# Attention of a hybrid decoder layer: copies, turns and scores in an interleaved order, and the 16-key meta tile's weighted sums as split fp32r products

## The reference

```python
score = jnp.einsum('bqhs,bqh->bqs', jax.nn.relu(logits), w_idx)      # indexer
_, sel = lax.top_k(score, topk)                                      # topk = 128 keys
s = jnp.einsum('bqhc,bqkc->bqhk', q_lat, kv_sel) * (ATT_HEAD_DIM ** -0.5)
p = jax.nn.softmax(jnp.where(valid, s, -jnp.inf), axis=-1)
o_lat = jnp.einsum('bqhk,bqkc->bqhc', p, kv_sel)
y_att = jnp.einsum('bthc,hcd->bthd', o_lat, w_uv)
```

## Time and profile before

| | us |
|---|---|
| median of 3 runs (range) | 1017.39 (1017.03 to 1017.8) |
| the profiled execution's own time | 1017.49 |
| its span in the trace | 1015.8 |
| PE busy | 996.9, 98% of the span |
| DVE, ACT, POOL busy | 714.0, 493.8, 118.1 |
| first score of the attention, first output product behind it | 529.5, 600.1 |

### The profile page before, as it was taken

The page is one execution under the profiler, slowest core; times in us unless marked ns, Lnnn a source line. Parts: engine busy times, 40 slices in busy tenths (PEclk is TensorE's granted clock), DMA queues, the critical chain, the costliest instruction groups (busy, mean ns, idle before and its releaser), DMA issues.

```text
span 1015.8 us, 18999 instructions
## 1 busy us (share of the span) xinstructions
PE 996.9 (98%) x7028; PEld 907.9 (89%) x7028; DVE 714.0 (70%) x1317; ACT 493.8 (49%) x868; POOL 118.1 (12%) x92
## 2 busy tenths in 40 slices
PE   9999999999999999999999999999999999999996
PEld 8999999999999988699765668889999999988886
DVE  6988888887322264699997523699989889942236
ACT  6656665566121264546346522576656665812121
POOL 0000000001121262045302205320000000000000
PEclk9999999999999999999999999999999999999999
DMA  7233332323223313132110102113323232333212
GB/s 252 84 100 107 102 105 90 116 80 105 86 86 111 113 44 116 36 123 82 44 42 1 43 1 83 43 42 126 124 83 124 85 121 96 125 103 101 98 57 84
DMA packets 30849, 90.48 MB, mean 89 GB/s; under 512 B 4689, under 2 KB 5329, under 8 KB 30801
## 3 DMA queue, kind: packets, MB, share of 16 engines
q1 hardware_dynamic: 30800, 89.83, 26.7%
HBM read 87.72 MB, written 2.10 MB: 88 GB/s over the span
## 4 chain that ended last, share of the span: by engine, by line
PE 81%; DVE 15%; ACT 2%; issue 1%; DMA 0%; SPq 0%; DVEq 0%; ACTq 0%
PE ps L1229 38%; PE ps L1287 22%; PE ps L1152 9%; DVE sc L2201 3%; DVE top L2200 3%; PE ps L1714 2%; PE ps L1424 1%; PE ps L1692 1%; DVE qk L2240 1%; PE ps L1705 1%; DVE wlo L1877 1%; PE ps L1489 1%; PE ps L1722 1%; PE ps L1337 1%; PE ps L1335 1%
## 5 line engine op out<-in xcount | busy, mean ns | idle before, releaser
L1229 PE MATMUL ps<-tsum,whi 128*128 128x264 f32 (+1 forms) x1280 | 243.1, 282 | 0.5 <-ACT ht L790 0.5
L1229 PEld LDWEIGHTS ps<-tsum,whi 128*128 128x128 f32 x1280 | 202.3, 188 | 0.7 <-issue 0.7
L1229 PE MATMUL ps<-tsum,wlo 128*128 128x264 f32 (+1 forms) x640 | 180.3, 282 | 0.0
L1229 PE MATMUL ps<-xh,whi 128*128 128x264 f32 (+1 forms) x480 | 135.4, 282 | 0.3 <-ACT sil L790 0.3
L1229 PE MATMUL ps<-xl,whi 128*128 128x264 f32 (+1 forms) x480 | 135.5, 282 | 0.0
L1229 PE MATMUL ps<-xh,wlo 128*128 128x264 f32 (+1 forms) x480 | 135.3, 282 | 0.0
L729 ACT ACTIVATE whi<-wraw 128x1408 fp32r<-128x1408 f32 (+1 forms) x48 | 74.6, 1555 | 123.0 <-PE ps L1287 123.0
L1787 DVE TENSOR_TENSOR wlo<-wraw,whi 128x1408 fp32r<-128x1408 f32 (+1 forms) x38 | 70.0, 1843 | 85.3 <-ACT whi L729 85.3
L1287 PE MATMUL ps<-hh,whi 128*128 128x264 f32 (+1 forms) x462 | 124.2, 323 | 0.0
L1287 PE MATMUL ps<-hh,wlo 128*128 128x264 f32 (+1 forms) x462 | 123.5, 322 | 0.0
L1287 PE MATMUL ps<-hl,whi 128*128 128x264 f32 (+1 forms) x462 | 123.4, 321 | 0.0
(11 more groups left out here) (287 smaller groups left out, 1828.0 us busy)
## 6 DMA issues: line engine op xcount, KB each, us to landing
wraw<-in_ffn_w_gate SPq DMA_DIRECT2D x43, 512.0 KB, 4.2
wraw<-in_ffn_w_up SPq DMA_DIRECT2D x42, 512.0 KB, 4.3
wraw<-in_ffn_w_down SPq DMA_DIRECT2D x32, 384.0 KB, 3.2
wraw<-in_ffn_w_down SPq DMA_DIRECT2D x32, 320.0 KB, 3.5
wraw<-in_w_in SPq DMA_DIRECT2D x19, 512.0 KB, 4.5
wraw<-in_w_out SPq DMA_DIRECT2D x8, 512.0 KB, 4.4
out<-zrow SPq DMA_DIRECT2D x8, 256.0 KB, 2.0
x<-in_x SPq DMA_DIRECT2D x3, 528.0 KB, 7.5
```

Source lines behind the costliest of these rows:

```text
L1229: mm = pe.matmul(ps[:, bank, 0:(HT, HALF_SEQ)[p // 2]], w[:, k * P:(k + 1) * P], v[:, k, :], start=(first and k == 0 and n == 0), stop=(k ...
```

## The change

**Order.** In all three `attention()` loops a round is cut finer: two scores, two turns, one score, the weigh of the meta tile, turn 2, one score, and then the other weighs and turns. ACT makes its copies of tiles 0 and 1 behind the exponentials of heads 0 and 1, that of tile 2 behind head 2, the rest behind head 3; DVE's copies move in the same way, `normalise` goes behind the third `masked`, and the mLSTM pieces and the late selection rounds go to a round's end.

**Meta tile.** Its weighted sum becomes a split product. The transposes of tile 0 take 32 key columns instead of 16 (`META_ROWS`); ACT copies the turned bank as fp32r into partitions 0 to 31 of `pt_h`, DVE subtracts that copy from the bank and puts the rest into partitions 32 to 63. PE makes one fp32r matmul with `clo` (low part of the latents) over 16 partitions, and one with `meta_c`, which holds the high part twice (partitions 0 to 15 and 32 to 47, zeros elsewhere), over 64 partitions. ACT makes `chi` once (16x128), POOL makes `clo` and `meta_c` once (`split_latents`). Tiles 1 to 4 stay plain fp32.

**Memory.** `c_parts` and `pts` lie over `cs` and `v1` with another type; two of the four score buffers move (`sbuf[2]`, `sbuf[3]`).

```diff
-HEAD_GATED = ((1, 0), (1, 1), (2, 1), (3, 1))
-HEAD_HI = ((1, 1), (2, 0), (3, 0), (4, 0))
+HEAD_GATED = (1, 1, 2, 3)
+HEAD_HI = (2, 2, 3, 4)
...
-LATE_AT = ((4, 0), (4, 1), (5, 0))
+LATE_AT = (4, 4, 5)
...
+META_ROWS = 32
...
-        sbuf = [sil[:, 0, :], sil[:, 1, :], pt_flat[:, 1024:1024 + T], pt_flat[:, 1024 + T:1024 + 2 * T]]
+        sbuf = [sil[:, 0, :], sil[:, 1, :], pt_flat[:, 2048:2048 + T], qk[:, 3, :]]
...
+                def split_latents():
+
+                    pool.wait_ge(c_hi, 1)
+                    pool.wait_ge(ct_turned, 1)
+                    m = N_META
+                    pool.tensor_tensor(clo[0:m, 0, :], cmat[0:m, 0, :], chi[0:m, 0, :].bitcast(F32), ALU.subtract).then_inc(c_lo, 1)
...
                 mix_lo(9)
+                split_latents()
                 causal_mask(3)
...
                 act.activation(ct[:, END[3]:T], ps[:, 5, 0:P], ACT.Copy).then_inc(ct_ready, 1)
+                act.activation(chi[0:N_META, 0, :], cmat[0:N_META, 0, :], ACT.Copy).then_inc(c_hi, 1)
                 hi(MIX0 + 4, 0, UW, False)
...
+                        if i and t % 2 == 0:
+                            continue
+                        act.wait_ge(pt_turned, t + 1)
+                        if t >= 2:
+                            act.wait_ge(pv_step, t - 1)
+                        dst, src = (pt[t % 2], ps[:, t % 2, :]) if i else (pt_h[t % 2][0:META_ROWS, :], ps[0:META_ROWS, t % 2, :])
+                        act.activation(dst, src, ACT.Copy).then_inc(pt_hi, 1)
...
                 def weigh(G, i):
                     t = TP0[G] + i
-                    pe.wait_ge(pt_even if t % 2 == 0 else pt_odd, t // 2 + 1)
-                    if i == 0 and G >= 1:
-                        pe.wait_ge(ol_ready, G)
-                    pe.matmul(ps[:, 3, :], cmat[0:ROWS[i], i, :], pt_flat[0:ROWS[i], (t % 2) * 512:(t % 2 + 1) * 512],
-                              start=(i == 0), stop=(i == 1 + G // 2)).then_inc(pv_step, 1)
+                    if i == 0:
+                        pe.wait_ge(pt_hi, copies_by_act(t))
+                        if G >= 1:
+                            pe.wait_ge(ol_ready, G)
+                        pe.wait_ge(c_lo, 3)
+                        m = N_META
+                        pe.matmul(ps[:, 3, :], clo[0:m, 0, :], pt_h[t % 2][0:m, :], start=True, stop=False)
+                        copied_weights(t)
+                        pe.matmul(ps[:, 3, :], meta_c[:, :], pt_h[t % 2][0:64, :], start=False, stop=False).then_inc(pv_step, 1)
+                        return
+                    copied_weights(t)
+                    pe.matmul(ps[:, 3, :], cmat[:, i, :], pt[t % 2], start=False, stop=(i == 1 + G // 2)).then_inc(pv_step, 1)
...
+                        turn(G - 1, 0)
+                        turn(G - 1, 1)
+                    if G < GROUPS:
+                        scores(4 * G + 2)
+                    if G >= 1:
+                        weigh(G - 1, 0)
+                        if last_tile >= 2:
+                            turn(G - 1, 2)
+                    if G < GROUPS:
+                        scores(4 * G + 3)
+                    if G >= 1:
+                        for i in range(1, last_tile + 1):
                             weigh(G - 1, i)
+                            if i + 2 <= last_tile:
+                                turn(G - 1, i + 2)
...
-                        if t % 2 == 0:
+                        if i == 0:
+                            dve.wait_ge(pt_hi, copies_by_act(t))
+                            ins = dve.tensor_tensor(pt_h[t % 2][32:32 + META_ROWS, :], ps[0:META_ROWS, t % 2, :],
+                                                    pt_h[t % 2][0:META_ROWS, :].bitcast(F32), ALU.subtract)
+                        elif t % 2 == 0:
```

More of the change, by code:

```diff
@@ L283, in build, with meta_turn, copies_by_act, copies_by_dve @@
         pt_flat = v1[:, :, :, :].rearrange("p j h v -> p (j h v)")
-        sbuf = [sil[:, 0, :], sil[:, 1, :], pt_flat[:, 1024:1024 + T], pt_flat[:, 1024 + T:1024 + 2 * T]]
+        sbuf = [sil[:, 0, :], sil[:, 1, :], pt_flat[:, 2048:2048 + T], qk[:, 3, :]]
+        pt_h = [pts[:, e * 512:(e + 1) * 512] for e in range(2)]
+        pt = [pt_flat[:, (2 + e) * 512:(3 + e) * 512] for e in range(2)]
+        def meta_turn(t):
+            return t in TP0
+        def copies_by_act(t):
+            return sum(meta_turn(v) or v % 2 == 1 for v in range(t + 1))
+        def copies_by_dve(t):
+            return sum(meta_turn(v) or v % 2 == 0 for v in range(t + 1))
         qk_flat = qk[:, :, :].rearrange("p c t -> p (c t)")
@@ L398, in build @@
         pt_turned = sem("pt_turned")
[L399 to L400 removed]
+        pt_hi = sem("pt_hi")
+        pt_lo = sem("pt_lo")
+        c_hi = sem("c_hi")
+        c_lo = sem("c_lo")
         pv_step = sem("pv_step")
@@ L1113, in attention @@
                         act.activation(olt[g], ps[:, 3, :], ACT.Copy).then_inc(ol_ready, 1)
+                        for h in range(ML_H):
+                            if HEAD_HI[h] == G:
+                                mlstm_hi(h)
                         if G == 4:
@@ L1734, in attention @@
                     last_tile = 1 + (G - 1) // 2
[L1735 to L1746, removed]
-                    if G >= 1:
-                        for i in range(last_tile + 1):
-                            if 2 <= i + 1 <= last_tile:
-                                turn(G - 1, i + 1)
+                    if G < GROUPS:
+                        scores(4 * G)
+                        scores(4 * G + 1)
+                    if G == 0:
+                        turn_mlstm((0, 1))
+                    if late is not None:
+                        project(late)
+                    if G >= 1:
+                        turn(G - 1, 0)
+                        turn(G - 1, 1)
+                    if G < GROUPS:
+                        scores(4 * G + 2)
[3 more added lines that the diff above has]
+                            turn(G - 1, 2)
+                    if G < GROUPS:
+                        scores(4 * G + 3)
+                    if G >= 1:
+                        for i in range(1, last_tile + 1):
                             weigh(G - 1, i)
+                            if i + 2 <= last_tile:
+                                turn(G - 1, i + 2)
                         if G in (1, 2):
@@ L2393, in attention @@
-                    if G >= 1:
-                        copy_even(G - 1, range(2, last_tile + 1))
+                    if G < GROUPS:
+                        masked(4 * G)
+                        masked(4 * G + 1)
+                    if G >= 1:
+                        copy_even(G - 1, (0, 1))
+                    if G < GROUPS:
+                        masked(4 * G + 2)
+                    if late is not None:
+                        normalise(late)
+                    if G >= 1 and last_tile >= 2:
+                        copy_even(G - 1, (2,))
@@ L2395, in attention @@
+                    if G < GROUPS:
+                        masked(4 * G + 3)
+                    if G >= 1:
+                        copy_even(G - 1, range(3, last_tile + 1))
+                    if G in (0, 2):
+                        normed_mlstm((2 + G // 2,))
+                    for h in range(ML_H):
+                        if HEAD_GATED[h] == G:
+                            gated_mlstm((h,))
+                    late_rounds(G)
+                    if G >= 1:
                         if late is not None:
```

78 lines of the change are left out of this document (38 added, 40 removed).

## The result

The changed kernel took 1025.97 us (median of 4 runs, 1025.39 to 1027.96), the kernel before beside it 1017.21 (1016.85 to 1017.8): a ratio of 1.009 [1.0076, 1.0105]. It is slower, as forecast, but by 8.8 us where 5.1 were said, and it lies 0.5 above the end of the range. The profiled execution took 1025.94 with a span of 1024.2, at a mean granted clock of 0.993 (before 0.998). The four executions of the changed kernel had means of 0.990 to 0.993.

The account below looks back on a forecast made before the run. PE, busy 98%, was taken to carry the end: 8.3 us of added idle less 3.2 saved gave about 5.05, plus 0.15 for ACT's copy, on 1017.49: 1022.7, said as 1022.5; range 1018.8 to 1025.5.

Parts of the forecast that it names:

- The clock: Rival, attention rounds 1 and 2: idling lowers PE's granted clock, doubling some 10 us of work at most, up to 1032; chance 0.02.
- The waits: PE's idle time in the attention's eight rounds, 3.5 us before and 11.8 after: +8.3, or +5.1 less the 3.2 saved.
- The meta product's saving: Eight meta weighs on PE: two fp32r matmuls of 0.33 replace 1.06 us, saving 0.40 each, 3.2 us in all.
- The moved mLSTM pieces: DVE's gated product and `normed_mlstm`, moved to the round's end: PE waits 0.6 us in round 1, 1.1 in round 2.
- The small terms: Outside the walk: ACT's 16x128 copy ahead of unit 4's split +0.15 us (0 to 0.3); POOL's four operations and wider turns nothing.
- PE's work decides: Rival in the attention: only PE's own instructions count, so the end moves by -3.2 us to 1014.2; chance 0.07.
- half the stalls vanish: Rival: rounds 3 to 8 end even, only rounds 1 and 2 lose, 3.3 us or less: 1018.5 to 1020; chance 0.13.
- no change: Rival: added idle of 3.2 us instead of 8.3 just pays for the saving, 1017.5; chance 0.05.
- The delays feed on each other: Rival in the attention: ACT's added 3 us push exponentials, these the next turns: +7 to +8 us, 1025; chance 0.05.

Follow-up runs that it names:

- with the clock held: Four idle 128x128 fp32 matmuls (fillers) added ahead of the meta pair in rounds 1 and 4 of the changed kernel; 1022.71 us, ratio 1.0046.
- the order alone: The new order of all three engines on the kernel before, meta tile's product left plain fp32; 1019.85 us, ratio 1.0032.
- the run that priced the shallow matmuls: 18 fp32r matmuls added behind the attention, on the changed kernel with idle matmuls in rounds 1 and 4 and mLSTM pieces back inside rounds; 1029.33 us, once.

## Why the prediction was off in size

The sum was 1017.49 + 5.05 + 0.15 = 1022.69; the profiled execution took 1025.94. Of the 3.25 between them 2.5 are the clock, 0.26 the waits less what the product saves, and 0.53 lie ahead of the attention (0.68 measured, 0.15 said); 0.04 went the other way.

- **The clock: 2.5 us, the step that failed.** The rival had been named, and set aside with "in pieces of 1.1 at most" and a chance of 0.02, in part because the trace of before shows no fall in the attention. In the changed kernel single waits of 1.02 and 1.21, with smaller ones beside them, stood ahead of the falls in both executions profiled, and the falls went when they were filled. The same paragraph said that rounds 1 and 2 would idle for a larger share than round 4 had, and still took that round's full clock as evidence. That was weak evidence whatever the share: round 4 of before had PE busy for 2.58 of 3.81 us in one part, as in the window ahead of the first fall, and its clock held (the windows stand at the end of this section). The bound, up to 1032, was too wide the other way: in the windows above the slow stretches are 4.17 us at 0.59 and 4.58 at 0.63, not two whole rounds.
- **The waits: +0.26, right.** 5.31 with the clock held, against 5.05; mechanism, places and sizes by round are shown. Nearly all of the 0.26 is round 8, where PE is at the second meta matmul 0.98 after the first (602.66 to 603.64) and not 0.74: DVE comes late to the subtraction. That the sum is so near is in part luck, as the next point shows.
- **The meta product's saving was mis-sized.** 0.33 a matmul was taken, 0.42 to 0.43 measured, so the pair saves 0.2 and not 0.4, 1.7 in all instead of 3.2. The error lay in reading the 0.10 between 0.43 and 0.53 as a price of shallowness, when it is half the price of changing depth. Each instruction of the plain pair has such a change on one side, each matmul of the new pair on both. It moved the sum little, as the prediction said: where the second matmul waits for the subtraction, it starts 0.71 after the first in round 6 (0.33 + 0.41 = 0.74 said), whatever the first one costs. Little is not nothing: the prediction gives 1.3 us for a matmul of 0.53 instead of 0.33, so 0.42 is worth some 0.6, and other pieces of the walk must have come out some 0.3 shorter than said to leave 0.26.
- **The moved mLSTM pieces** were priced inside rounds 1 and 2, at 0.6 and about 1.1; putting them back made these rounds 0.68 and 1.11 shorter and round 3 0.32 longer, 1.47 in all.
- **The small terms.** ACT's 16x128 copy, the term of the earlier trace rows, stood for 0.15. In the changed kernel it holds ACT for 0.20 until the next start:

```profile
426.69 0.29 ACT L1010 ACTIVATE c_parts<-cs 16x128 fp32r<-16x128 f32 x1
426.89 1.90 ACT L764 ACTIVATE whi<-wraw 128x2048 fp32r<-128x2048 f32 x1
```

The first score is 0.68 later than before, but 0.57 of that is there at 385 us already, ahead of every changed instruction. Over the runs of this study that start lies between 529.44 and 532.33 for kernels that are alike up to 426. So at most 0.1 of the 0.68 can be the change, and the rest is spread of single executions. POOL's four operations were hidden, as said: done at 495.9, and the mask behind them began at 496.4 and waited for DVE.

Of the other rivals, "PE's work decides", "half the stalls vanish" and "no change" are excluded by the stretch of 75.83 at full clock. "The delays feed on each other" is excluded by round 5 (+0.27 in the changed kernel, +0.28 with fillers) and round 6 (+1.45 in both).

What stays open is the rule by which the clock falls. The runs give filling the waits as a means that held it, and cases on both sides. Here are three windows after which it did not fall: round 4 of before, round 4 of the order alone, and round 2 of the changed kernel with fillers in rounds 1 and 4.

```profile
555.34:559.15 3.81, 2.58 (x9) 0.98 (x8) 3.64 (x12) 2.67 (x7) 1.27 (x1) 1.00 0.00 0
554.49:558.30 3.81, 2.36 (x12) 1.12 (x10) 3.27 (x11) 2.32 (x6) 1.27 (x1) 1.00 0.00 0
541.73:546.30 4.57, 2.80 (x8) 1.04 (x6) 2.95 (x12) 3.03 (x10) 0.00 (x0) 1.00 0.00 0
```

Ahead of the falls of the changed kernel it was 2.58 of 3.81 and 2.88 of 4.57, though where such a window is cut matters (2.32 of 3.81 from 533.42 to 537.23). What settles it is that the same work of round 6 was followed by a fall in one execution and by none in another: PE's busy time just ahead does not decide it alone.

## What to carry to other kernels

When a change spreads short waits over an engine that was nearly always busy, add up the idle share round by round, give a falling clock a real chance where it grows, and price it from rows. A trace without falls is weak evidence even for gaps like its own. Put useful work (or, to measure, idle work) into the wait before anything else is concluded from the new order. And price a matmul by its neighbours, not from the mean of a merged row: in this kernel a shallow one between deep ones costs more than padding it with zeros to their depth.

## What the runs showed of the hardware that was not expected

- Idle work can shorten a kernel: eight fp32 matmuls more (7044 instructions on PE against 7028), 2.5 us less in the attention.
- A change of depth between neighbouring matmuls costs 0.20 us at 512 columns of fp32r (0.43 by turns against 0.23 inside a row), half of it on either side; shallowness alone costs nothing. On a plain fp32 weigh it is 0.20 (1.06 against 0.86), and some 0.35 with the neighbours.
- The clock can differ between two executions of the same instructions: after the same work in round 6 it fell in one (0.56) and held in the other (1.00).
- The clock also fell where nothing waited. In the run that priced the shallow matmuls it was down from the last of the eighteen on (610.29), though PE had been busy without a gap since 604.99; windows of PE over the turns and over the output products behind them:

```profile
608.16:609.40 1.24, 1.24 (x4) 0.54 (x3) 0.00 (x0) 0.00 (x0) 0.00 (x0) 1.00 0.00 0
611.00:612.00 1.00, 1.00 (x3) 0.83 (x3) 0.00 (x0) 0.00 (x0) 0.00 (x0) 0.50 0.00 0
```

The output products from 611.61 on take 0.43 each instead of 0.24 until 613.7. It is one execution; that the shallow matmuls brought the fall, and by which property, is not shown.
